# Recurrent head pairs: the state step as two 64x64 products, the second head's inside products crosswise

## The reference, cut to what matters

```python
def rwkv7_scan(r, w, k, v, a_, b_):
    ...
    def step(state, inp):
        r_t, w_t, k_t, v_t, a_t, b_t = inp
        sa = jnp.einsum('bhij,bhj->bhi', state, a_t)
        state = state * w_t[:, :, None, :] + sa[..., None] * b_t[:, :, None, :] + v_t[..., None] * k_t[:, :, None, :]
        return state, jnp.einsum('bhij,bhj->bhi', state, r_t)
```

## Time and profile before

| | |
|---|---|
| runs | 2911.47, 2911.92, 2911.98 us |
| median | 2911.92 us |
| profiled execution, from first to last instruction (span) | 2909.9 us |
| its own time | not listed apart; the median lies 2.0 us over its span |
| mean granted TensorE clock | 0.998 of full speed |
| the eight pairs' recurrence | 206 to 566 us of the span |
| busy in 206.3 to 566 | TensorE 357.42, VectorE 269.35, ScalarE 149.40, GpSimd 103.43 us of 359.7 |

### The profile page before, as it was taken

One profiled execution on the slowest core, in us unless ns is written; L12 is line 12 of the kernel. 1 busy time (PEld: TensorE's weight loads), 2 busy tenths in 40 slices (PEclk: granted clock), 3 DMA queues, 4 the chain that ended last, 5 costly groups with the idle time before them and its releaser, 6 DMA issues.

```text
span 2909.9 us, 49401 instructions
## 1 busy us (share of the span) xinstructions
PE 2892.3 (99%) x19658; PEld 2423.8 (83%) x19658; DVE 1572.7 (54%) x2227; ACT 1103.5 (38%) x1673; POOL 1584.3 (54%) x1912
## 2 busy tenths in 40 slices
PE   9999999999999999999999999999999999999998
PEld 7877777788888888888888898888898888988887
DVE  5467877524556666775334265445763441473635
ACT  4454434333443322443433343233443342342323
POOL 6432233355646666677444557565584444565654
PEclk9999999999999999999999999999999999999999
DMA  5211111332426777533222323232333222232232
GB/s 173 94 45 41 42 55 45 97 141 95 130 82 217 252 273 254 179 113 126 85 89 73 95 87 113 87 109 87 106 124 115 77 88 87 87 102 94 94 102 73
DMA packets 92292, 322.21 MB, mean 111 GB/s; under 512 B 10144, under 2 KB 14368, under 8 KB 91808
## 3 DMA queue, kind: packets, MB, share of 16 engines
q1 hardware_dynamic: 84544, 302.39, 31.7%
q10 hardware_dynamic: 7520, 16.67, 1.7%
HBM read 315.09 MB, written 3.93 MB: 110 GB/s over the span
## 4 chain that ended last, share of the span: by engine, by line
PE 98%; issue 1%; DVE 1%; POOL 1%; DMA 0%; ACT 0%; POOLq 0%; SPq 0%; ACTq 0%; DVEq 0%
PE bank L906 25%; PE bank L910 25%; PE bank L907 25%; PE bank L1254 2%; PE bank L899 2%; PE bank L901 2%; PE bank L900 2%; PE bank L1265 2%; PE bank L1273 1%; PE bank L934 1%; PE bank L936 1%; PE bank L935 1%; PE bank L958 1%; PE bank L960 1%; PE bank L1785 1%
## 5 line engine op out<-in xcount | busy, mean ns | idle before, releaser
L837 POOL TENSOR_TENSOR w_lo<-w_raw,w_hi 128x256 fp32r<-128x256 f32 x1736 | 1419.2, 852 | 986.9 <-ACT w_hi L1862 980.5
L906 PE MATMUL bank<-act,w_hi 128*128 128x512 f32 (+1 forms) x3464 | 1312.7, 379 | 4.7 <-POOL w_lo L837 2.6
L910 PE MATMUL bank<-act,w_lo 128*128 128x512 f32 (+1 forms) x3464 | 1292.4, 373 | 0.0
L907 PE MATMUL bank<-act,w_hi 128*128 128x512 f32 (+1 forms) x3464 | 1291.4, 373 | 0.0
L906 PEld LDWEIGHTS bank<-act,w_hi 128*128 128x128 f32 x3464 | 652.9, 188 | 126.1 <-issue 8.3
L910 PEld LDWEIGHTS bank<-act,w_lo 128*128 128x128 f32 x3464 | 652.6, 188 | 115.2
L907 PEld LDWEIGHTS bank<-act,w_hi 128*128 128x128 f32 x3464 | 653.4, 189 | 106.7
L1862 ACT CAST w_hi<-w_raw 128x1024 fp32r<-128x1024 f32 (+1 forms) x438 | 454.4, 1043 | 345.1 <-DMA w_raw<-in_weights 163.6
L1870 ACT ACTIVATE arena<-bank 128x512 f32<-128x512 f32 (+1 forms) x177 | 104.3, 593 | 418.2 <-PE bank L910 401.6
L855 POOL TENSOR_TENSOR stats<-stats,exponent 128x8 f32<-128x8 f32 (+2 forms) x38 | 46.6, 1226 | 302.5 <-DVE stats L2914 150.0
L2600 DVE TENSOR_TENSOR act<-tmp,act 128x512 fp32r<-128x512 f32 (+1 forms) x140 | 121.2, 866 | 77.3 <-ACT act L1889 72.7
(11 more groups left out here) (359 smaller groups left out, 3087.4 us busy)
## 6 DMA issues: line engine op xcount, KB each, us to landing
w_raw<-in_weights SPq DMA_DIRECT2D x471, 512.0 KB, 3.5
arena<-in_ada SPq DMA_DIRECT2D x96, 512.0 KB, 5.0
arena<-in_strips ACTq DMA_DIRECT2D x8, 448.0 KB, 3.7
arena<-in_x ACTq DMA_DIRECT2D x1, 2048.0 KB, 10.9
y_scratch<-tmp ACTq DMA_DIRECT2D x7, 256.0 KB, 2.0
arena<-y_scratch ACTq DMA_DIRECT2D x1, 1792.0 KB, 8.1
arena<-in_dft ACTq DMA_DIRECT2D x2, 777.5 KB, 4.2
arena<-in_x SPq DMA_DIRECT2D x3, 512.0 KB, 7.4
```

The lines of the kernel that those rows point to most:

```text
L837: ins = nc.gpsimd.tensor_tensor(w_lo[:, k, cols], weights_of(u)[:, cols], w_hi[:, k, cols].bitcast(F32), ALU.subtract)
L906: nc.tensor.matmul(o, wh, xh, start=first, stop=False)
L907: nc.tensor.matmul(o, wh, xl, start=False, stop=False)
L910: mm = nc.tensor.matmul(o, wl, xh, start=False, stop=last)
```

## The change

The state step becomes two 64x64 products, one per head, in the two diagonal quarters, and `MCX` keeps the diagonal blocks alone (64 columns a chunk; the clearing at the start goes, VectorE fills it in one operation). In `values_inside` head 0 stays in the diagonal quarters and head 1 goes to the other two: its tokens of half r land in half 1 - r of its bank (`HALVES[r ^ h]`). The order becomes both heads' first terms, then both heads' second terms. `values_of_states` follows with the same halves. ScalarE puts head 1's halves back: three copies take the place of one, and the square is then made from the copy in SBUF.

```diff
-        MCX = take(NC, P)
+        MCX = take(NC, CH)
+        take(NC * CH)
...
                 for d in range(NC // 2):
                     for h in range(2):
-                        for rows in HALVES:
-                            nc.tensor.matmul(o[rows, h, CH * d:CH * (d + 1)], RBB[rows, d, 2 * h, :], TAZ[rows, d, h, CH:P],
-                                             start=d == 0, stop=False, skip_group_check=True)
                         for r, rows in enumerate(HALVES):
-                            mm = nc.tensor.matmul(o[rows, h, CH * d:CH * (d + 1)], MRK[rows, d, h, :], VT_[rows, d, h, :],
-                                                  start=False, stop=2 * d + r == 0, skip_group_check=True)
+                            nc.tensor.matmul(o[HALVES[r ^ h], h, CH * d:CH * (d + 1)], RBB[rows, d, 2 * h, :],
+                                             TAZ[rows, d, h, CH:P], start=d == 0, stop=False, skip_group_check=True)
+                    for h in range(2):
+                        for r, rows in enumerate(HALVES):
+                            mm = nc.tensor.matmul(o[HALVES[r ^ h], h, CH * d:CH * (d + 1)], MRK[rows, d, h, :],
+                                                  VT_[rows, d, h, :], start=False, stop=2 * d + r == 0, skip_group_check=True)
...
-                                mm = nc.tensor.matmul(o[rows, h, CH * d:CH * (d + 1)], ARs[p % 2][from_rows, c, 1, :],
+                                mm = nc.tensor.matmul(o[HALVES[r ^ h], h, CH * d:CH * (d + 1)], ARs[p % 2][from_rows, c, 1, :],
                                                       state(c)[from_rows], start=False, stop=True, skip_group_check=True)
...
-                    mm = nc.tensor.matmul(b[:, 0, CH * c:CH * (c + 1)], MCX[:, c, :], state(c), start=True, stop=True)
+                    for rows in HALVES:
+                        mm = nc.tensor.matmul(b[rows, 0, CH * c:CH * (c + 1)], MCX[rows, c, :], state(c)[rows], start=True,
+                                              stop=True)
...
-                done(nc.scalar.activation(by_token(YSQ.rearrange("p (d h s) -> p d h s", h=2, s=CH)), in_columns("Y", p, CH),
-                                          ACT.Square), "rw_ysq")
-                copied("Y", by_token(YT.rearrange("p (d h s) -> p d h s", h=2, s=CH)), in_columns("Y", p, CH))
+                y, o = YT.rearrange("p (d h s) -> p d h s", h=2, s=CH), in_columns("Y", p, CH)
+                nc.scalar.activation(y[:, :, 0, :], o[:, 0], ACT.Copy)
+                nc.scalar.activation(y[HALVES[0], :, 1, :], o[HALVES[1], 1], ACT.Copy)
+                nc.scalar.activation(y[HALVES[1], :, 1, :], o[HALVES[0], 1], ACT.Copy).then_inc(sem("rw_emptied_a"), 1)
+                emptied(act, "Y", p)
+                done(nc.scalar.activation(YSQ, YT, ACT.Square), "rw_ysq")
...
-            do(V_.memset(MCX, 0.0))
...
-                def state_map(r, signal="vector_step"):
-                    do(V_.tensor_tensor(by_head(MCX[r, :, r]), rm[r, :, :, CH:P], mask(ident_c)[r], ALU.add), signal)
+                def state_map():
+                    do(V_.tensor_tensor(by_head(MCX), rm[:, :, :, CH:P], mask(ident_c), ALU.add), "rw_mcx")
...
-                state_map(HALVES[0])
-                state_map(HALVES[1], "rw_mcx")
+                state_map()
```

More of the change, by code:

```diff
@@ L1308, in values_of_states @@
                     for h, from_rows in enumerate(HALVES):
-                        for r, rows in enumerate(HALVES):
+                        for r in range(2):
                             c = 2 * d + r
                             if c:
-                                mm = nc.tensor.matmul(o[rows, h, CH * d:CH * (d + 1)], ARs[p % 2][from_rows, c, 1, :],
+                                mm = nc.tensor.matmul(o[HALVES[r ^ h], h, CH * d:CH * (d + 1)], ARs[p % 2][from_rows, c, 1, :],
                                                       state(c)[from_rows], start=False, stop=True, skip_group_check=True)
```

## The result

| | before | after |
|---|---|---|
| median, us | 2911.92 | 2915.59 |
| range of 21 runs each, us | 2911.47 to 2912.72 | 2915.27 to 2917.45 |
| span of the profiled execution, us | 2909.9 | 2913.3 |

The ratio is 1.0013, with a 95% interval of 1.0007 to 1.0019: 3.7 us slower, within the 0.2% that had been set as no change that counts, but with an interval that leaves out one. The forecast was 2914.3 us, with a range of 2908.5 to 2919.5.

A forecast was written before the change was run, and what follows sets the result against it. TensorE, busy 99% of the span, was taken as the bound. Per pair 0.84 - 0.06 - 0.88 = -0.10 us, plus a 0.45 wait in seven pairs: +2.35 us, 2914.3 us on the median, range 2908.5 to 2919.5.

The forecast's parts named there:

- a step, L910 to L907: TensorE between weight blocks around one state step in quarters: 0.92 us, where it was 0.69 (0.77 with a wait).
- steps 1 to 5 together: TensorE's state steps per pair: steps 2 to 5 cost +0.84 us, step 1 -0.06 without its late state map.
- last step, up to the first inside product: Step 6 on TensorE: 0.32 us to come, 0.17 until its quarters take the next block; 0.49, change 0.
- inside products in, from T: TensorE finishes the inside products at T + 1.09 us; 64 records take 0.92 in place of 1.80, -0.88.
- T: Start of the first record of the last state step on TensorE, from which the prediction measured times.
- `decayed_b` ends, from T: VectorE's scaled key for the next pair, made after the last step is emptied, ends at T + 1.44 us.
- `removals` starts, from T: Next pair's first group on TensorE gets VectorE's key at T + 1.54 us.
- a pair, all in all: Steps and inside products sum to -0.10 us a pair; with +0.45 wait +0.35 in seven, the eighth -0.10.
- The rival without overlap: Inside products do not overlap in the banks; -0.88 and the wait go, +6.2 us, 2918.1; chance 7%.
- The wait: TensorE idles before the next pair's removals for VectorE's scaled keys: +0.45 us in seven pairs, bounds 0 and 0.9.
- the hand-over: From VectorE's finished key to TensorE's removals: 0.10 us, an estimate.
- ScalarE: Three copies of 0.38 us, overlapping by 0.10, take 0.94, no later than today's 1.09; cost 0.

The follow-up runs named there:

- `after_keys`: Changed kernel with VectorE making decayed_a right after unit_keys and decayed_b before the last state step; 2910.93 us, ratio 0.9996.
- `steps_only`: Changed kernel with crosswise inside products and ScalarE's copies taken back, so only state steps go to quarters; 2918.95 us, ratio 1.0021.
- `inside_keys_last`: As `inside_keys`, with state step 6 alone as two 64x64 products directly ahead of the inside products; 2904.47 us, ratio 0.9973.
- `inside_keys`: Kernel before with only inside products crosswise, ScalarE's copies, and VectorE's decayed_a moved to right after unit_keys; 2904.64 us, ratio 0.9974.
- `after_slot_first`: Changed kernel with TensorE's wait for the slot of group aB moved ahead of its waits for the two keys; 2914.94 us.

## Why the prediction was right

It was right in sign and mechanism, and near in size. That the total came within 1.3 us is in part luck, as the end of this section shows. By its own terms, per pair and read from the fourth:

| term | predicted, us | measured, us |
|---|---|---|
| a step, L910 to L907 (now L911 to L908) | 0.92 | 0.91 to 0.93 |
| steps 1 to 5 together | +0.78 | +0.81 |
| last step, up to the first inside product | 0.49 | 0.36 (380.83 to 381.19) |
| inside products in, from T | 1.09 | 1.07 (`after_keys`, nothing to wait for: 379.40 to 380.47) |
| `decayed_b` ends, from T | 1.44 | 1.46 |
| `removals` starts, from T | 1.54 | 1.69 (load), 1.72 (product) |
| a pair, all in all | +0.35 | +0.51 to +0.53 in the first six |

- **The steps** are right to 0.01 us each: an unseen group of four records could be built from a larger one, which means that coming and going cost the same here as around 32 records. `steps_only` has the same cost a step without the rest of the change.
- **The inside products** run in four quarters: the 64 records start between 381.19 and 382.21, 16 ns each against 28 before. The rival without overlap falls, and with it what the Trainium skill ("TensorEngine Tiling (Array Packing)", Restrictions and Gotchas) says of one bank and two row tiles, as a matter of time: each of the two banks takes products from both input halves, into different partitions, and if these had to take turns in a bank, no record could come sooner than 28 ns after the one before (a quarter takes one every 56, and there are two banks). The Trainium skill ("TensorEngine Tiling (Array Packing)", Tiling Modes, Key Properties) also says that a change of tiling mode drains the array; the runs agree, since the step costs 0.23 us more where it changes the shape and, in `inside_keys_last`, 0.08 less where it does not.
- **The wait** is there, in seven pairs, for the reason given; `inside_keys` and `after_keys` take it away and get 4.9 and 4.7 us for it. Its size was the term that was most off: `removals` starts 0.15 us later than forecast in six pairs. VectorE was where it had been put (1.46 for 1.44); the hand-over was taken as 0.10, as from a product to VectorE, and is 0.23, since the wait for the slot, long fulfilled, stands in TensorE's queue behind the late one. `after_slot_first` moves it ahead and brings the hand-over to 0.12. In the seventh pair `decayed_b` ends only at T + 1.84, and the load starts at T + 2.06: the prediction took all pairs to be like the fourth within 0.02 us, but VectorE is later in this one (in the kernel before, too: there `decayed_b` ended at T + 1.76, against 1.57 in the fourth). Why is open.
- **ScalarE** was costed at nothing and cost nothing, though its copies overlapped less than assumed.

**The total, and where luck comes in.** What the recurrence costs is read from the starts of the same weight block in the two traces. Before: the blocks behind `values_of_states` of the fourth and of the eighth pair, and between them TensorE's one wait for VectorE's L3053, in the eighth pair.

```profile
382.10 0.50 PE L906 MATMUL bank<-act,w_hi 128*128 128x512 f32 x1
...
548.10 0.69 PE L1254 MATMUL bank<-arena 64*64 64x64 f32 x32 [0.39 <-DVE arena L3053]
...
565.59 0.50 PE L906 MATMUL bank<-act,w_hi 128*128 128x512 f32 x1
```

After, the same two blocks:

```profile
383.96 0.50 PE L907 MATMUL bank<-act,w_hi 128*128 128x512 f32 x1
...
568.65 0.50 PE L907 MATMUL bank<-act,w_hi 128*128 128x512 f32 x1
```

The block is 1.86 us later in the fourth pair and 3.06 later in the eighth. The changed kernel came to the recurrence 0.21 us early (a block that started at 205.46 starts at 205.25), so the recurrence costs 3.27 us more, where 2.35 was forecast. Each of the first six pairs is 0.16 to 0.18 over its forecast, and the seventh, with its longer wait, 0.3. The eighth gives back 0.51 where 0.10 was forecast: it has no next pair to wait for, as forecast, but the wait of 0.39 us at 548.10 is gone too, as in every kernel here with all steps in quarters, and the prediction did not count it. Behind the recurrence another 0.6 us is lost at one place (last section), and 0.2 us is won at the very start and again at the very end. So the total was missed by only 1.3 us because a wait that was put too small and a place that was not looked at were in part made up for by gains that nobody had forecast.

`inside_keys` beats both kernels: 7.5 us under the one before, and the interval of its ratio (0.9963 to 0.9985) leaves out one. The change had one part that pays and one that costs, and left the paying part waiting.

## What to carry to other kernels

Count a small group by what it takes to enter and leave its shape of the array, 0.23 us for a lone step here, and not by its columns: moving it to idle quarters pays where it stands beside groups of the same shape, and costs where it stands between full-array products. When a stretch of the bounding engine becomes shorter, look for what was finished just in time behind it, and move that work first; here one engine's order, with an idle gap to fill, was worth as much as the change itself. Where an engine waits for several things in a row, put the wait that ends last behind the others: one that stood behind it cost 0.11 us a time here.

## What the runs showed beside this

- A wait that is long fulfilled still costs 0.11 us when it stands behind the late one (0.23 against 0.12 us from VectorE's end to TensorE's load, in all seven pairs of one trace each).
- The first inside products started 0.03 us after the step before them, and 0.16 in `steps_only`, where they need the step's own quarters: quarters take their work independently even across groups.
- Some 0.6 us of the changed kernel's loss lie outside the recurrence. In its trace one VectorE operation of the cross attention takes 0.91 us where its sisters take 0.35, and TensorE waits 0.55 us for it (VectorE, then TensorE):

```profile
782.36 0.35 DVE L3276 TENSOR_SCALAR arena<-arena 128x256 f32<-128x256 f32 x1
...
782.94 0.91 DVE L3276 TENSOR_SCALAR arena<-arena 128x256 f32<-128x256 f32 x1
```

```profile
783.91 1.09 PE L1621 MATMUL bank<-table,arena 128*128 128x128 f32 x8 [0.55 <-DVE arena L3276]
```

The traces of the four kernels with all steps in quarters (the changed one, `steps_only`, `after_keys`, `after_slot_first`) have this delay at that place, 0.6 us each, and those of the six others have not. Why is open; no run tested it, and the prediction had nothing on this stretch.
